# Experts' gate and up weights loaded in two halves of each partition's rows, each half given back on its own

## What is computed

```python
scores = sigmoid(xt @ w_router)
_, idx = top_k(scores + b_router, 8)
gate = sel / sum(sel) * 2.5
def block_step(acc, blk):           # a block of 64 tokens of one expert e
    tok, w, e = blk
    xb = xt[tok]
    h = silu(xb @ w_e1[e]) * (xb @ w_e3[e])      # w_e1, w_e3: 1024 x 256
    yb = (h @ w_e2[e]) * w[:, None]              # w_e2: 256 x 1024
    return acc.at[tok].add(yb), None
y = layer_norm(ALPHA * h + shared + routed)
```

## Time and profile before

| | us |
|---|---|
| median of 3 runs (2052.11 to 2059.55) | 2056.1 |
| the profiled execution's own time | 2052.74 |
| its span, first to last instruction | 2051.0 |
| PE busy in the span | 1804.3 (88%) |
| gate/up products of the experts (line 1942), 2048 records | 517.8 |
| idle of PE before them, ended by expert weights | 150.3 |
| down products (line 1960), 1024 records | 233.8 |
| share of q1 (loads issued by SP) of sixteen DMA engines over the span | 60.6% |
| mean granted clock of PE over the span | 0.943 |

### The profile page before, as it was taken

The page is one execution under the profiler, slowest core; times in us unless marked ns, Lnnn a source line. Parts: engine busy times, 40 slices in busy tenths (PEclk is TensorE's granted clock), DMA queues, the critical chain, the costliest instruction groups (busy, mean ns, idle before and its releaser), DMA issues. The chain is left out here.

```text
span 2051.0 us, 28955 instructions
## 1 busy us (share of the span) xinstructions
PE 1804.3 (88%) x10578; PEld 1052.1 (51%) x10578; DVE 628.6 (31%) x1490; ACT 385.2 (19%) x915; POOL 362.8 (18%) x529
## 2 busy tenths in 40 slices
PE   7999996888999997999888887988888888888887
PEld 6857766887778883473333333433333333333332
DVE  1387745774214312242111111111111111111127
ACT  0115543442120101111111111111111111111102
POOL 1000002888850000001111111111010101110100
PEclk9999998999999999999999899999898989998998
DMA  3443312011243325139999999999999999999976
GB/s 116 143 137 102 104 31 47 3 34 35 67 148 97 87 57 206 75 140 420 420 421 413 416 412 412 408 418 408 404 409 398 410 398 406 408 413 400 407 295 253
DMA packets 160782, 532.04 MB, mean 259 GB/s; under 512 B 22061, under 2 KB 88927, under 8 KB 110205
## 3 DMA queue, kind: packets, MB, share of 16 engines
q1 hardware_dynamic: 138971, 488.63, 60.6%
q0 software_dynamic: 20640, 41.23, 5.4%
q10 hardware_dynamic: 1098, 1.18, 0.2%
HBM read 522.52 MB, written 41.42 MB: 275 GB/s over the span
## 5 line engine op out<-in xcount | busy, mean ns | idle before, releaser
L1942 PE MATMUL bank<-arena 128*64 128x512 f32 x2048 | 517.8, 664 | 152.0 <-DMA arena<-in_w_e 150.3
L1942 PEld LDWEIGHTS bank<-arena 128*64 128x64 f32 x2048 | 160.1, 152 | 508.5 <-issue 507.0
L1960 PE MATMUL bank<-arena 128*64 128x512 f32 x1024 | 233.8, 598 | 0.0
L2134 DVE TENSOR_TENSOR arena<-bank,arena 128x256 f32<-128x256 f32 x64 | 27.2, 425 | 601.2 <-ACT arena L2006 601.2
L1824 POOL DMA_INDIRECT arena<-h_rows,index x66 | 66.9, 1013 | 775.7 <-DVE index L2025 728.5
L1422 PE MATMUL bank<-arena 128*128 128x276 f32 x768 | 184.7, 399 | 7.3 <-ACT arena L1524 3.1
L1422 PEld LDWEIGHTS bank<-arena 128*128 128x128 f32 x768 | 146.4, 191 | 41.7 <-ACT arena L1524 3.5
L1201 PE MATMUL bank<-arena 64*64 64x64 f32 (+2 forms) x2816 | 126.3, 245 | 27.5 <-DVE arena L1314 14.7
L2006 ACT ACTIVATE arena<-bank 128x256 f32<-128x256 f32 x64 | 24.7, 386 | 621.0 <-PE bank L1942 621.0
L1201 PEld LDWEIGHTS bank<-arena 64*64 64x64 f32 x2816 | 111.0, 140 | 34.3 <-DVE arena L1314 15.8
L1960 PEld LDWEIGHTS bank<-arena 128*64 128x64 f32 x1024 | 67.8, 136 | 110.9 <-issue 109.7
(11 more groups left out here) (323 smaller groups left out, 1840.0 us busy)
## 6 DMA issues: line engine op xcount, KB each, us to landing
arena<-in_w_e SPq DMA_DIRECT2D x384, 1024.0 KB, 14.8
arena<-in_w_in SPq DMA_DIRECT2D x50, 512.0 KB, 4.2
arena<-routed_rows SPq DMA_DIRECT2D x8, 2048.0 KB, 23.2
arena<-in_w_mem_kv SPq DMA_DIRECT2D x4, 1024.0 KB, 5.9
arena<-in_cache_mem_k SPq DMA_DIRECT2D x8, 512.0 KB, 4.6
arena<-in_cache_mem_v SPq DMA_DIRECT2D x8, 512.0 KB, 5.4
arena<-in_w_out SPq DMA_DIRECT2D x2, 2048.0 KB, 11.3
arena<-in_w_s SPq DMA_DIRECT2D x3, 1024.0 KB, 10.5
```

What stands on the lines that cost most here:

```text
L1942: mm = pe.matmul(p_gu[t * S:(t + 1) * S, :], xt[:, v, c, t * S:(t + 1) * S], w13[2 * v + t][:, :, c, :], start=(c == 0), stop=(c == KD - 1))
L1960: mm = pe.matmul(p_y[h][t * S:(t + 1) * S, :], hidT[:, j, t * S:(t + 1) * S], w2[2 * v + t][:, j, h * 512:(h + 1) * 512], start=(j == 0), ...
```

## The change

Each gate/up load is split in two of 4 KB a partition: half 0 carries chunks 0 to 3 of each partition (the first four of its eight rows), half 1 chunks 4 to 7. Each half has its own semaphores for arrival (`expert_w13_0_v`, `expert_w13_1_v`), and PE waits for a half just ahead of its four chunks. After the first four chunks PE signals the new `s_gu0`, upon which SP issues the four half-0 loads of pair n+2; the half-1 loads follow after `s_gu`, the down loads after `s_y` as before. Bytes, products and their order are the same.

```diff
-def load_w13(sp, m, io, e, buf, sem):
+def load_w13(sp, m, io, e, buf, half, sem):
     w = m.at(O_WEXP[buf], 3, 2 * D)
     for x, name in enumerate(("w_e1", "w_e3")):
         src = io[name][0][ds(e, 1)].rearrange("e (p c) n -> p (e c n)", c=KD)
-        sp.dma_start(w[:, x, :], src).then_inc(sem, 16)
+        sp.dma_start(w[:, x, half * D:(half + 1) * D], src[:, half * D:(half + 1) * D]).then_inc(sem, 16)
 def prefetch_expert(sp, m, io, e):
-    load_w13(sp, m, io, e, e, m.sem(f"expert_w13_{e // 2}"))
+    for half in range(2):
+        load_w13(sp, m, io, e, e, half, m.sem(f"expert_w13_{half}_{e // 2}"))
     load_w2(sp, m, io, e, e, m.sem(f"expert_w2_{e // 2}"))
...
             def load(r, done, v, e):
+                sp.wait_ge(s_gu0, NP * r + done + 1)
+                for t in range(2):
+                    load_w13(sp, m, io, e + t, 2 * v + t, 0, s_w13[0][v])
                 sp.wait_ge(s_gu, NP * r + done + 1)
                 for t in range(2):
-                    load_w13(sp, m, io, e + t, 2 * v + t, s_w13[v])
+                    load_w13(sp, m, io, e + t, 2 * v + t, 1, s_w13[1][v])
...
-                        pe.wait_ge(s_w13[v], (64 * NP // 2) * r + 64 * i + 64)
                         pe.wait_ge(s_xt, NP * r + n + 1)
-                        for c in range(KD):
-                            for t in range(2):
-                                mm = pe.matmul(p_gu[t * S:(t + 1) * S, :], xt[:, v, c, t * S:(t + 1) * S],
-                                               w13[2 * v + t][:, :, c, :], start=(c == 0), stop=(c == KD - 1))
+                        for half in range(2):
+                            pe.wait_ge(s_w13[half][v], (64 * NP // 2) * r + 64 * i + 64)
+                            for c in range(KD // 2 * half, KD // 2 * (half + 1)):
+                                for t in range(2):
+                                    mm = pe.matmul(p_gu[t * S:(t + 1) * S, :], xt[:, v, c, t * S:(t + 1) * S],
+                                                   w13[2 * v + t][:, :, c, :], start=(c == 0), stop=(c == KD - 1))
+                            if half == 0:
+                                mm.then_inc(s_gu0, 1)
                         mm.then_inc(s_gu, 1)
```

More of the change, by code:

```diff
@@ L1741, in stage_mix_experts @@
     s_yv, s_ya = sem("output_scaled_vector"), sem("output_scaled_scalar")
-    s_w13 = [sem(f"expert_w13_{v}") for v in range(2)]
+    s_w13 = [[sem(f"expert_w13_{half}_{v}") for v in range(2)] for half in range(2)]
+    s_gu0 = sem("pair_half_products")
     s_w2 = [sem(f"expert_w2_{v}") for v in range(2)]
```

## The result

The changed kernel takes 2090.7 us (median of four, 2080.6 to 2094.5) against 2054.9 before: 1.0164 times as long, 95% interval 1.0139 to 1.0188. Run once more on another occasion it took 2084.8, 1.014 (1.0105 to 1.0175). I had forecast 2071 and a range of 2052 to 2086. The sign is right, the size isn't: 30 to 36 us were added, not 15. In the profiled executions the loop over the experts, from its first gate/up product to the end of its last, takes 1055.6 us before and 1092.3 and 1096.8 in the two of the change.

A forecast was written before the change was run, and what follows sets the result against it. The trailing DMA engine's own work was taken to set the loop's period, 16.66 us a pair. Terms +19.8 + 2.0 − 3.5 − 3.0 = +15.3 us on the 2056.1 median gave 2071 us, range 2052 to 2086.

The forecast's parts named there:

- rival A: Expert loop: issuing 3.5 us earlier fills the DMA holes, up to 16 us comes back, 2055 us; chance 0.17.
- (1): Gate/up loads in the loop: 1984 8 KB packets an engine become 3968 of 4 KB, 10 ns each, +19.8 us.
- (2): Semaphore packets of the loop's 248 further loads, one more small packet each on every engine: +2.0 us.
- Rival C: Gate/up loads: reading half of a partition's 8 KB costs 20 ns a packet, +38.7 us, 2095 us; chance 0.10.
- rival B: Gate/up loads: the extra packet costs little, 6 ns or less, 2056 to 2063 us; chance 0.12.
- D: Rival on the loop's loads: each costs a fixed time, 0.3 us for 248 loads, 74 us, 2145 us; chance 0.02.
- (3): Start of the loop: first refill issued 3.5 us earlier, in the middle of the first product, −3.5 us.
- (4): End of the loop: only half the last pair's products remain behind the last weights' landing, −3.0 us.
- (5): New waits of PE and SyncE and fuller issue queue in the loop: nothing, at most taking back 3.5 us.

The follow-up runs named there:

- fillers: An 8-byte-a-partition load added behind each gate/up load of the kernel before: 2076.5 us (1.0109); of the kernel with spread slots: 2049.3 us (0.998).
- spread slots: Kernel before with filled token slots spread over partitions, so gathered and scattered rows fall evenly on DMA engines: 2031.8 us; same on the changed kernel: 2047.1 us.
- throttled: Changed kernel with SyncE's waits moved later, so each group of loads is issued later and its queue never fills: 2073.8 us (1.0098).
- ScalarE's queue: Changed kernel with half 1 of the gate/up weights issued by ScalarE instead of SyncE: 2066.4 us (1.0062); with crowded slots too: 2104.1 us.
- late halves: Changed kernel with the early give-back undone, both halves issued after the whole product, 4 KB packets kept: 2089.0 us (1.0179).
- crowded slots: Kernel before with filled slots laid to crowd on few DMA engines, the same always trailing: 2095.3 us (1.0209); same on the changed kernel: 2150.1 us (1.0434).

## Why the prediction was right and wrong

**The bound: right.** Trailing engines, not the mean of sixteen, set the period. Putting 131 rows each way on them cost 42 us, as rows times 0.16 us had it. Taking rows off gave 21 us. That is within what I had expected, but not rows times 0.16 us: 109 rows each way would be 35, and even engines were then full (idle 0.2%), so that the mean had become the bound. It ran at 420 GB/s with its holes gone though nothing was issued earlier. So rival A (fill the holes by earlier issue) was wrong from its root: the holes come from uneven engines.

**(1) and (2), packets: right, my 10 ns at the upper end.** Even engines: 15.4 = packets + small packets − 6.5. The fillers price a tiny packet at 7.8 ns, so 248 semaphore packets cost 1.9 us, and 20.0 us are left for 1984, 10.1 ns each; I had taken 10. Other measures of the same price are lower. The slices with spread slots stand at 421 GB/s before and 414 after for nearly the whole loop, which is about 8 ns a packet. The difference of their loops, 10.3 us instead of 15.4, gives 7.5 with the same 6.5. The throttled kernel, with its later start (6.2 us) and the gain at its end taken out, gives 7.5 as well, and the one with ScalarE's queue, whose last product still stands whole behind its landing, 7. By the median packets of the traces it is 2 x 159 − 309 = 9 ns. So it is 7 to 10 ns. Rival C (20 ns for reading half of 8 KB) is out, since all these kernels read so; rival B (6 ns) lies just below. The Trainium skill's three cycles (DMA: Bandwidth & Descriptors, Why small descriptors are slow), which gave 7 us where 14 to 20 were measured, are too low for this stream. D, a fixed time for each load, is out as well: it asked for 74 us, and the throttled kernel has the 248 extra loads and pays 19.5. (The 2.0 us fixed that D quotes from the Trainium skill stand on that page for a DMA issued by GpSimd and not under Bandwidth; SyncE issues these.)

**(3) and (4), start and end: right** by the timelines above, 3.4 us each. The late halves, without the gain at the start, were no slower than the change beyond the noise, so no total time shows it.

**(5), the new waits: this is the step that failed.** "An issue held back by a full queue leaves engines with work, so I put this at nothing." I had the row that warned of it, and could have counted that the loads of two pairs go from 108 descriptors an engine to 180, and I priced it at no more than 3.5 us. It cost 15 to 21 us: 30 to 36 us measured for the change, 15.3 of them in the sum. The runs show what it takes. Even engines with a full queue: +15.4. Uneven engines without one: +12 (ScalarE's queue), +19.5 (throttled, of which 6 us are its later start). Uneven engines and a full queue: +30 to 36, with crowded slots +55, and with half as many gate/up loads of twice the size +69. Either alone adds little or nothing to the packets' price; together they do, and the more, the more uneven the engines are.

The first half of my sentence holds on the mean: the engines were idle for 1.5% of the time before and 1.3% after. The conclusion doesn't. What I had left out is that an engine with work can be slow at it: 4.0% of the large packets were long instead of 1.7%, and their excess, 24 us an engine more in 900 us, makes up what was missing (22 to 26 us by the loops of the profiled executions, 37 and 41 less 15.3). I had expected that the engines ahead run dry behind a full queue and that their restarts cost. There is something in it, since 13% of the packets that start while fewer than all engines are busy are long, against 3% of the others. But some seven in ten long packets start with all sixteen busy, so that a restart of the engine itself accounts for few of them. What makes a packet long, and why a full queue before uneven engines makes more of them, isn't shown by any of these runs. Nor is it shown why the fillers, with as many descriptors but SyncE less held up, had few more of them (2.6%) and lost only 4 us. These two stay open.

**The version that beats both.** The kernel before with spread slots, 2031.8 us, 0.9908 (0.9884 to 0.9932). Half loads gain nothing on top of it, they cost 15.

## What to carry to other kernels

Where DMA engines are saturated, ask which of them lands last and what it carries that the others don't. Balancing it was worth more here than any earlier issue, and a mean share of 99.9% hid it. Before splitting loads, count the descriptors that can be outstanding on an engine against the most that could be outstanding without an issue growing long; if they will be more and the engines are uneven, split over two queues or issue later. The count alone isn't enough: the fillers had the same 180 and lost little. Look at the issues' median, and at the times of single packets beside the mean share. Giving back a buffer early gains only where a queue would otherwise be empty, here at the two ends of the loop.

## What the runs showed of the hardware

- A packet has a fixed part of 7 to 10 ns in a saturated stream: 10.1 ns for each 8 KB split in two by the medians of the pair with spread slots, 8 by its rates of 421 and 414 GB/s, and 7.8 ns for a packet of 8 bytes.
- A saturated stream can lose its rate with all engines busy: with uneven engines and a full queue, 4.0% of the large packets (8.0% with crowded slots) took over 1.25 times the usual 159 or 309 ns, with even engines and a full queue 0.4%.
- Count 9 descriptors an engine for each load (8 packets and the semaphore's) and at most two pairs of loads outstanding (6 loads a pair before, 10 after; 14 in all in the throttled kernel). With at most 108 descriptors an engine SyncE's issues never grew (gate/up loads, longest 0.69 us); with at most 126 few did (median 0.38, longest 2.55 us); with up to 180 most did (median 1.01, longest 6.9 us). The fillers also come to 180, and there the median was 0.45 us, the longest 4.8. How many the queue really held wasn't measured.
- ScalarE's queue holds its own: with at most 72 descriptors there its longest issue took 0.68 us while SyncE's, with at most 108, was nearly free (median 0.38, longest 3.4).
- Products of two experts that alternate between the two halves of a bank's partitions took 7.09 us, the same 32 records one expert after the other 12.24.
